# A decoder step on one NeuronCore: three moves around the first pair of sample attention

## The reference

```
mod = silu(c) @ w_ada + b_ada                      # six modulation vectors
q, kc, vc, ks, vs, kw, vw, g, hc, bg, cg = split(modulate(x) @ w_in)
gates = sigmoid(g)                                 # three branches a head
# sample tokens, per sequence: 2048 past keys in 16 pages of 128, behind a page table
p_cmp = softmax(q . compressed keys);  choose 16 of 32 blocks of 64 keys by importance
o = gates . (p_cmp @ vc,  softmax(q . chosen keys) @ v,  softmax(q . last 512 keys) @ v)
y = bg * conv3(cg * hc)                            # short convolution
x = x + g1 * (concat(rmsnorm(o), rmsnorm(y)) @ w_o)
x = x + g2 * swiglu(modulate(x))
```

## Time and profile before

| | us |
|---|---|
| median of 3 runs (888.61 to 890.68) | 890.17 |
| the profiled execution | 891.03 |
| its span, first to last instruction | 889.2 |
| TensorE busy in the span | 846.4 |
| VectorE busy | 626.1 |
| ScalarE busy | 374.3 |
| GpSimd busy | 306.1 |

### The profile page before, as it was taken

How to read it: one execution, slowest core, us unless ns; L and a number is a source line. 1 busy time by engine, 2 the same in 40 slices (tenths; PEclk the granted TensorE clock), 3 DMA queues, 4 the chain that set the end, 5 groups by cost and what they waited for, 6 DMA issues and landing times.

```text
span 889.2 us, 16417 instructions
## 1 busy us (share of the span) xinstructions
PE 846.4 (95%) x6333; PEld 728.1 (82%) x6333; DVE 626.1 (70%) x1232; ACT 374.3 (42%) x754; POOL 306.1 (34%) x303
## 2 busy tenths in 40 slices
PE   3898999999989899999999989999999999999998
PEld 2776788999975667667677989999999999888886
DVE  3457773698758876685759898888999888434434
ACT  1242342221235447668625744444444445322320
POOL 6776100000022314445001167777777772000000
PEclk9899999999997999999999999999999999999999
DMA  8999622264468993961021914333333326222201
GB/s 234 353 372 393 233 64 90 71 216 163 147 230 328 399 370 118 310 181 42 1 65 78 237 49 123 100 96 91 93 92 95 90 95 211 95 95 95 77 1 53
DMA packets 89164, 138.83 MB, mean 156 GB/s; under 512 B 9268, under 2 KB 59988, under 8 KB 84799
## 3 DMA queue, kind: packets, MB, share of 16 engines
q1 hardware_dynamic: 74866, 96.26, 33.6%
q0 software_dynamic: 9376, 40.31, 12.3%
q10 hardware_dynamic: 4844, 1.21, 0.7%
HBM read 130.58 MB, written 11.31 MB: 160 GB/s over the span
## 4 chain that ended last, share of the span: by engine, by line
PE 78%; DVE 7%; DMA 5%; POOL 4%; issue 3%; ACT 3%; SPq 0%; DVEq 0%; ACTq 0%; POOLq 0%
PE bank L2453 19%; PE bank L2455 19%; PE bank L2454 19%; PE bank L2447 4%; POOL arena L894 3%; PE bank L2809 2%; DMA wring<-in_w_ada 2%; PE bank L2521 2%; PE bank L2941 2%; PE bank L2463 2%; PE bank L2462 2%; PE bank L2482 2%; PE bank L2973 2%; PE bank L2779 1%; DMA arena<-in_cache_k_slc,idx 1%
## 5 line engine op out<-in xcount | busy, mean ns | idle before, releaser
L2453 PE MATMUL bank<-s,ring_hi 128*128 128x288 f32 x620 | 184.6, 298 | 3.2 <-DVE ring_lo L537 3.2
L2454 PE MATMUL bank<-s,ring_lo 128*128 128x288 f32 x620 | 183.6, 296 | 0.0
L2455 PE MATMUL bank<-s,ring_hi 128*128 128x288 f32 x620 | 183.1, 295 | 0.0
L2453 PEld LDWEIGHTS bank<-s,ring_hi 128*128 128x128 f32 x620 | 116.9, 189 | 3.9 <-DVE ring_lo L537 3.8
L2455 PEld LDWEIGHTS bank<-s,ring_hi 128*128 128x128 f32 x620 | 117.5, 189 | 0.0
L2454 PEld LDWEIGHTS bank<-s,ring_lo 128*128 128x128 f32 x620 | 117.1, 189 | 0.0
L537 DVE TENSOR_TENSOR ring_lo<-mem,ring_hi 128x512 fp32r<-128x512 f32 x84 | 108.3, 1325 | 0.9 <-POOL mem L990 0.5
L537 DVE TENSOR_TENSOR dn_w<-wring,dn_w 128x2048 fp32r<-128x2048 f32 (+1 forms) x11 | 23.1, 2096 | 65.9 <-ACT dn_w L534 65.9
L903 POOL DMA_INDIRECT arena<-in_cache_k_slc,idx x8 | 7.9, 990 | 159.8 <-PE bank L2455 151.7
L2453 PE MATMUL bank<-dn_w,dn_hi 128*128 128x512 f32 x160 | 62.2, 389 | 0.0
L2454 PE MATMUL bank<-dn_w,dn_lo 128*128 128x512 f32 x160 | 62.2, 389 | 0.0
(11 more groups left out here) (450 smaller groups left out, 2119.3 us busy)
## 6 DMA issues: line engine op xcount, KB each, us to landing
wring<-in_w_gu SPq DMA_DIRECT2D x44, 512.0 KB, 5.2
wring<-in_w_ada SPq DMA_DIRECT2D x16, 1024.0 KB, 10.3
wring<-in_w_in SPq DMA_DIRECT2D x10, 1024.0 KB, 5.2
wring<-in_w_down SPq DMA_DIRECT2D x10, 1024.0 KB, 5.1
wring<-in_w_ada SPq DMA_DIRECT2D x16, 512.0 KB, 8.7
proj<-in_x_prompt SPq DMA_DIRECT2D x4, 512.0 KB, 6.2
mem<-in_state_k_win POOLq DMA_DIRECT2D x8, 256.0 KB, 5.6
mem<-in_state_v_win POOLq DMA_DIRECT2D x8, 256.0 KB, 7.9
```

Source lines behind the costliest of these rows:

```text
L2453: pe.matmul(dst, sh, ml, start=first and k == 0, stop=False)
L2454: pe.matmul(dst, sl, mh, start=False, stop=False)
L2455: ins = pe.matmul(dst, sh, mh, start=False, stop=last and k == len(pairs) - 1)
```

## The change

Three moves. On VectorE, the eviction of the convolution's last half comes ahead of the second page's turn, and the two additions go between the last two evictions. The four instructions of the gates go from the end of the convolution group into the second pair (gp = 1), behind norm_apply(11) and ahead of turn_window(2). On TensorE, the first modulation step of group 2 goes from the end of the first pair to behind scores(0). No instruction is added or removed.

```diff
@@ -1863,7 +1863,10 @@
                     key = ("cv", 2, m, h)
                     if m == 3 and h:
-                        turn_page(0, 1)
+                        dve.wait_ge(y_square, 3)
+                        for x in range(2):
+                            dve.tensor_tensor(hcT[:, x + 1, :], hcT[:, x + 1, :], hcT[:, x, :], ALU.add).then_inc(y_summed, 1)
+                            dve.wait_ge(y_summed, x + 1)
                     want_filled(dve, key)
@@ -1884,15 +1887,8 @@
                     cmp_groups(0)
-                    dve.wait_ge(gate_exp, 2)
-                    for z in (gat[:, 0:96], gat[0:TS, 96:120]):
-                        link(dve.tensor_scalar(z, z, 1.0, None, ALU.add))
-                        link(dve.reciprocal(z, z))
                     turn_page(0, 0)
-                    dve.wait_ge(y_square, 3)
-                    for x in range(2):
-                        dve.tensor_tensor(hcT[:, x + 1, :], hcT[:, x + 1, :], hcT[:, x, :], ALU.add).then_inc(y_summed, 1)
-                        dve.wait_ge(y_summed, x + 1)
+            turn_page(0, 1)
             evac(("kTn",), kTn, ps(("kTn",))[:, 0:128].rearrange("p (x n) -> p x n", x=2))
@@ -2024,6 +2020,10 @@
                 if gp == 1:
                     norm_inverse(2)
                     norm_apply(11)
+                    dve.wait_ge(gate_exp, 2)
+                    for z in (gat[:, 0:96], gat[0:TS, 96:120]):
+                        link(dve.tensor_scalar(z, z, 1.0, None, ALU.add))
+                        link(dve.reciprocal(z, z))
@@ -2847,6 +2847,7 @@
             scores(0)
+            ada_step(2, 0)
             turn_blocks(1)
@@ -2864,7 +2865,7 @@
-                    for kk in range(2 * gp, 2 * gp + 2):
+                    for kk in range(max(1, 2 * gp), 2 * gp + 2):
                         ada_step(2, kk)
```

## The result

| | before | after |
|---|---|---|
| median of 19 runs each, us | 891.57 (888.61 to 894.04) | 893.17 (891.01 to 898.14) |
| ratio, after to before | | 1.0022 (95%: 1.0011 to 1.0032) |
| span of the profiled execution, us | 889.2 | 891.3 |

The changed kernel is slower by some 2.0 us (0.0022 x 891.57; 1.0 to 2.9 by the interval); the two medians themselves differ by 1.60 us. The first three runs of before had a median of 890.17; with more of them it is 891.57.

A forecast was written before the change was run, and what follows sets the result against it. VectorE was taken as the bound up to 301 us, then a key gather nearly level with it. Terms -1.25 - 0.78 + 0.6 - 0.34 + 1.56 gave -0.2; with the clock's 1.8, +1.6 us on 890.17: 891.8 us, range 888.9 to 894.2.

The forecast's parts named there:

- First move: VectorE at the convolution's end, gates gone and evictions reordered: first importance starts at 263.75 instead of 265.00, gain 1.25 us.
- Second move: Modulation step behind the first scores: the second importance comes earlier and VectorE's wait for it ends, gain 0.78 us.
- its transfer: 1 MB of weights issued early near 273 us delays the second pair's second key page, loss 0.6 us (bounds 0 and 2.4).
- The wait for the second page's gather: Sign at the second pair: VectorE's second page turn shows a wait for its key gather.
- The later key page: Key gather landing at 307.3 us comes 1 to 3 us earlier and no longer bounds, gain 0.34 us.
- Third move: Gates ahead of turn_window(2) and L1806 in the second pair delay the third pair's scores and VectorE's masks, loss 1.56 us.
- The clock: TensorE's hole ahead of the third pair's scores widens to 3.6 us, its clock falls to half, loss 1.8 us (0 to 3.4).
- All four signs: Third pair: TensorE idle about 2.7 us in one piece, granted clock 0.5, scores 4 us, no TensorE wait for L1806.
- The hole costs nothing: Rival: clock stays full at the gates' hole, total -0.2 us, 890.0 us; chance 0.27.
- More holes: Rival: second hole of 2 to 3 us at 279 to 282, another fall costing up to 3.4 us, 894.8 us; chance 0.15.
- Faster: Rival: full clock and the key page unhindered, 889.4 to 888.4 us; chance 0.08.

The follow-up runs named there:

- after_again: The changed kernel (after) measured once more, nothing edited, in a later group of runs; 893.74 us, 1.0016 to before.
- gates_only: Before with only the gates moved into the second pair, the other two moves left out; 893.1 us, 1.0015 to before.
- behind_again: Repeat of gates_behind, unedited, in a later group of runs; 891.55 us, 0.9988 to before.
- gates_in_wait: After with the gates put ahead of the first pair's masks, where VectorE waits for the first scores; 891.88 us, 0.9999 to before.
- warm_hole: After with five discarded matmuls of constants on TensorE ahead of the third pair's scores; 892.88 us, 1.0011 to before.
- reorder_only: Before with only VectorE's new order of additions, evictions and second page at the convolution's end; 889.74 us, 0.9980 to before.
- warm_all: gates_in_wait plus 3, 2 and 2 discarded matmuls ahead of the first importance, the second, and the third pair's scores; 891.93 us, 0.9995 to before.
- undo_gates: After with the gates back at their old place ahead of the first page, the other two moves kept; 890.41 us, 0.9990 to before.
- gates_behind: After with the gates still in the second pair, but behind the window's turn and the importance's copy and mask; 891.75 us, 1.0013 to before.
- step_only: Before with only the modulation step moved behind the first scores; 890.12 us, 0.9985 to before.
- warm_hole3: After with three discarded matmuls of constants on TensorE ahead of the third pair's scores; 892.82 us, 1.0005 to before.
- undo_warm: undo_gates plus 2, 1 and 1 discarded matmuls ahead of the first importance, the second, and the third pair's scores; 890.89 us, 0.9985 to before.

## Why the prediction was right, and where it was off

The forecast was +1.6 us and 891.8; measured are +2.0 us and 893.17. The difference of the two absolute values is mostly before's own median, which rose by 1.4 us with more runs. The ratio 1.0022 lies just outside 0.2%, where the forecast, 1.0018, lay just inside; the interval, 1.0011 to 1.0032, takes in both. That the total fits so well is in part luck. Counted from the base, the profiles differ by 2.7 us (after) and 1.85 us (after_again) at the fourth importance, not by 1.6, and after had won 0.76 us ahead of the base by nothing in the change. The steps can be checked at the four importances.

**First move: 1.25 us.** L2648 starts at 263.06, which is 263.82 by before's base (foreseen 263.7 to 263.9). At the copy behind it the gain is 1.18 us (10.76 to 9.58), and 1.40 in after_again. Its parts came out too: the second half waits 0.83 us for the last product (foreseen 0.65), the new keys do not wait. But it is not the same in every execution: in those that show the low clock during the last convolution products (gates_only, behind_again, gates_in_wait, warm_hole) the first importance comes at 10.9 to 11.1 us.

**Second move: 0.78 us; its transfer: -0.6.** VectorE's wait for the importance is gone, and TensorE waits there instead. Together with the first move that was 1.43 us (1.25 + 0.78 - 0.6) at the second importance; measured 1.69 and 1.52. The wait for the second page's gather, which was to show, did not come in after: VectorE turned it without a wait. SyncE's queue shows the 1 MB where it was expected (the row joins it with the second 1 MB, issued from 279.64 on):

```profile
272.87 7.58 SPq L720 DMA_DIRECT2D wring<-in_w_ada  x4
```

The gathers of the two pages took 9.8 and 11.1 us from their issue (265.06 and 266.37), so they landed at 274.9 and 277.4. The first, 8.9 us in before, became 0.9 us longer. The second landed 23.3 us after the base and VectorE came for it at 23.55. The rule of the Trainium skill that a DMA engine takes a packet from each queue in turn ("DMA: Bandwidth & Descriptors", "Queues, rings and completion order") would have made this wait near 2.4 us by the prediction's estimate. The traces neither show that nor exclude sharing. In after the cost was 0 for VectorE; in after_again it waits 0.60 us for the first page and 0.78 for the second:

```profile
276.42 2.31 DVE L1832 STREAM_TRANSPOSE mem<-arena 128x2048 f32<-128x2048 f32 x1 [0.60 <-DMA arena<-in_cache_k_slc,idx]
279.51 2.31 DVE L1832 STREAM_TRANSPOSE hbuf<-arena 128x2048 f32<-128x2048 f32 x1 [0.78 <-DMA arena<-in_cache_k_slc,idx]
```

But the early transfer is not needed for such a wait. gates_only and reorder_only do not have it, their second page took 11.0 and 11.3 us as well, and VectorE waits 0.82 and 0.25 us for it. What goes with the wait is the first pair's scores: it comes in seven of the eight profiles in which these took 2.35 to 3.67 us (not in warm_all), and in none of the six in which they took over 4 us. So the term of 0.6 us is not shown as a cost of the transfer. The later key page was no bound any more, as foreseen (308.18 without a wait, where before waited 0.35).

**Third move: 1.56 us.** Right in kind and a little small: with the gates ahead of the copy the third stage was 19.33 to 19.62 us in all five profiles, and in the nine others 17.00 to 18.18, mean 17.65. That is 1.8 us. The surplus over 1.56 has no single cause. In after TensorE pauses for 0.90 us "issue" at 286.75, in the middle of the second pair's values, and VectorE waits 0.77 us behind it, where it waited 0.39 in before (a wait that the prediction's list between 277 and 304 us leaves out). The pause was not foreseen. In after_again there is none, and VectorE waits 1.10 us for slower scores instead.

**The clock: 1.8 us, the term that decided.** All four signs that were named for it came: one idle piece of 2.77 us, a granted clock of 0.50, scores of 4.08 us, and no wait of L1806 for TensorE. VectorE's waits rose by 1.74 (1.96 - 0.22) and 0.79 us. The second part is the values, slower as well (4.22 us), which the prediction named and did not count, so the term was too small for this execution: 18.13 - 15.68 = 2.45 us, or 2.8 with the page's 0.34 us that was won back. For after_again it is 1.2 us (16.91) and 1.6. So 1.8 lies between the two executions that were looked at, and its exact size is luck.

**What was wrong in the reasoning** is the comparison. (A small slip besides: in the earlier trace rows the clock's low digit stands in slice 13 alone, not in 13 and 14.) It took before as a kernel without a fall at this place, from one profile. Of the seven profiles with the old hole of 1.20 us and no added matmuls (before, undo_gates, gates_behind, behind_again, gates_in_wait, reorder_only, step_only) four have a fall in the scores (3.17 to 3.83 us); of the three with the wide hole all have it (3.83 to 4.08); of the four with added matmuls none. With the wide hole the fall comes earlier (0.8 us and 1.7 us ahead of the first score and 0.05 us behind it, against 0.2 to 1.4 us behind it) and lasts longer in two of three (6.8 us, against 3.4 in all others). That it also comes more often is not shown by three of three against four of seven, and the hole is not the only thing that causes one. And over whole executions after's mean granted clock was no lower than before's (the median over the runs is 0.989 for after, and 0.987, 0.988 and 0.987 for before in its three groups). What the move costs by the clock in the median run is the difference of two frequencies that 14 profiles can't give. The gates' own part rests on the third stage, which parts the five profiles from the nine others, that of the clock on warm_hole3's profile and on timed runs that do not part.

**Rivals.** "The hole costs nothing" falls: both profiles of after show the fall, and the ratio is above 1. "More holes" is not seen in after's first profile, but in after_again the second pair's scores took 3.65 us behind a wait of 2.52 us for VectorE, the second hole that this rival described, with the waits for the key pages ahead of it; the stage of the hole took 0.4 us more (18.24 against 17.85) and the one with the slower scores 0.2 more (19.55 against 19.33), not up to 3.4. This rival's sum is also off on paper: +1.6 + 1.8 + 1.5 is 4.9, and 895.1 in place of 894.8. "Faster" is excluded by the interval.

**A better version.** reorder_only, at 0.9980, is the only kernel whose interval stays clear below 1 by more than 0.0001, and both undo_gates and reorder_only beat after by more than their intervals. That they beat before by more than 0.2% is not shown.

## What to carry to other kernels

An instruction that nobody needs soon is still not free where it stands ahead of one that another engine waits for: put it behind the copy that frees the bank, not ahead of it (the third stage was 1.75 us shorter in gates_behind than in after, and 1.53 in behind_again than in after_again). The timed runs do not settle it: 0.9988 against 1.0016 for after_again, and 1.0013 against 1.0022 for after, both with intervals that overlap. When a pause is to hide work, ask what makes the pause: if it is the low clock of the engine that is waited for, it is gone in the executions in which the clock is full. And gains need not add: each alone, the first two moves gave 1.8 and 1.3 us, and 0.9 together. Check each against the landing of the next page before summing them, though here the page explains it in one profile only.

## What the runs showed of the hardware that was not expected

- The same kernel draws its clock falls differently from execution to execution. In after's two profiles the second pair's scores took 2.35 and 3.65 us, the third's 4.08 and 3.83, and the first's 4.09 and 3.67, while the single runs of after spread over 7 us.
- A fall came behind a hole of only 1.20 us (undo_gates, clock 0.53 in 300.8 to 304.2), with the scores already under way at full clock; in other executions the same hole brought none. The Trainium skill, "TensorE: Matmul & The Clock Gate", "What's actually happening", has it that throttled is the default and activity releases it. The added matmuls agree with that: with TensorE busy 6.41 of 7.00 us the clock stayed full. The stretches are of warm_hole3 and of after, both from 4.2 us ahead of the third pair's scores on; in after TensorE was busy 3.64 us of 7.00:

```profile
295.00:302.00 7.00, 6.41 (x92) 2.98 (x93) 6.12 (x27) 0.51 (x3) 1.15 (x2) 1.00 1.01 413
```

```profile
297.00:304.00 7.00, 3.64 (x64) 1.62 (x75) 5.64 (x26) 0.51 (x3) 1.15 (x2) 0.75 1.01 412
```

- TensorE paused for 0.45 to 1.32 us in the second pair's values in eight of fourteen profiles, with no releaser that the profile names, and not for a value page (the two gathers, issued at 261.30 and 262.61 in after, took 6.4 us). In seven the pause is behind the 50th of the 64 matmuls; in undo_warm it is behind the 44th:

```profile
285.56 1.31 PE L2785 MATMUL bank<-arena,hbuf 128*64 128x128 f32 x20 [0.97 <-issue]
```

undo_warm has three added matmuls ahead of it, six records. So all eight stop at the same place of TensorE's list, behind the 1834th matmul record of the trace, and not at the same matmul. In each of the eight, TensorE goes on 1.3 to 1.5 us after the end of a packet of 16 KB in the DMA queue that the page calls "instruction" (in after the packet ends at 286.26 and TensorE goes on at 287.65; in undo_warm 284.28 and 285.56). In the six without a pause TensorE reaches the place no earlier than that: 1.3 us after the packet's end in before, 1.9 us or more in the others. This looks like a wait for its own instructions, but no run tested it.
- Filling a hole with discarded matmuls restores the clock and buys next to nothing in time: 1.0005 against 1.0016 for after_again, 0.9985 against 0.9990 for undo_gates, each within the other's interval.
